# Two of the four sums of weight blocks of a seven-product group, by accumulating DMA transfers in place of VectorE

## What is computed

```
def swiglu(x, g, w_gate, w_up, w_down):
    n = rms_norm(x, g)
    return (jax.nn.silu(n @ w_gate) * (n @ w_up)) @ w_down
```

## Time and profile before

| | us |
|---|---|
| median of 3 runs | 1427.65 (1426.31 to 1430.56) |
| profiled execution, its own time | 1429.83 |
| its span | 1428.5 |
| TensorE busy | 1402.7 (98%) |
| weight loads of TensorE busy | 1321.5 (93%) |
| VectorE busy | 1061.1 (74%) |
| ScalarE busy | 713.0 (50%) |
| POOL busy | 156.6 (11%) |

### The profile page before, as it was taken

The page is one execution under the profiler, slowest core; times in us unless marked ns, Lnnn a source line. Parts: engine busy times, 40 slices in busy tenths (PEclk is TensorE's granted clock), DMA queues, the critical chain, the costliest instruction groups (busy, mean ns, idle before and its releaser), DMA issues.

```text
span 1428.5 us, 24281 instructions
## 1 busy us (share of the span) xinstructions
PE 1402.7 (98%) x9340; PEld 1321.5 (93%) x9340; DVE 1061.1 (74%) x1875; ACT 713.0 (50%) x1414; POOL 156.6 (11%) x110
## 2 busy tenths in 40 slices
PE   7999999999999999999999999999999999999998
PEld 6897878999999999999988978699999999999998
DVE  5658667878789889877444776677797998998853
ACT  5458555334355455454444685643344544544534
POOL 2416020210000000000222341102000000000002
PEclk9999999999999999999999999999999999999999
DMA  5330221233022222322233211213221223222312
GB/s 171 109 113 14 74 70 39 81 104 104 30 89 66 89 84 74 104 89 74 74 84 107 85 56 47 77 42 102 79 74 60 82 71 114 62 88 89 111 45 96
DMA packets 148642, 115.25 MB, mean 81 GB/s; under 512 B 17936, under 2 KB 143248, under 8 KB 148496
## 3 DMA queue, kind: packets, MB, share of 16 engines
q1 hardware_dynamic: 148528, 113.71, 26.4%
HBM read 108.90 MB, written 6.62 MB: 81 GB/s over the span
## 4 chain that ended last, share of the span: by engine, by line
PE 86%; DVE 7%; ACT 3%; DMA 1%; issue 1%; SPq 1%; DVEq 0%; ACTq 0%
PE ps L675 23%; PE ps L1359 13%; PE ps L1360 13%; PE ps L1361 13%; PE ps L802 3%; PE ps L804 3%; PE ps L803 3%; PE ps L1236 1%; PE ps L1127 1%; ACT pw L1521 1%; PE ps L728 1%; DMA wraw<-w_uq 1%; DVE ringl L2507 1%; PE ps L917 1%; PE ps L1153 1%
## 5 line engine op out<-in xcount | busy, mean ns | idle before, releaser
L2037 DVE TENSOR_TENSOR wlo<-wraw,whi 128x1024 fp32r<-128x1024 f32 (+2 forms) x87 | 97.6, 1122 | 122.9 <-ACT whi L1475 122.8
L1360 PE MATMUL ps<-tl,ringh 128*128 128x320 f32 x576 | 177.8, 309 | 0.0
L1361 PE MATMUL ps<-tth,ringl 128*128 128x320 f32 x576 | 177.5, 308 | 0.0
L1359 PE MATMUL ps<-tth,ringh 128*128 128x320 f32 x576 | 177.0, 307 | 0.0
L1891 ACT ACTIVATE ringh<-sums 128x512 fp32r<-128x512 f32 (+1 forms) x208 | 123.7, 595 | 106.3 <-DVE sums L2499 35.9
L2507 DVE TENSOR_TENSOR ringl<-sums,ringh 128x512 fp32r<-128x512 f32 (+1 forms) x208 | 134.2, 645 | 9.6 <-ACT ringh L1891 8.2
L1475 ACT ACTIVATE whi<-wraw 128x1024 fp32r<-128x1024 f32 (+2 forms) x87 | 81.0, 936 | 112.5 <-PE ps L675 52.0
L1360 PE MATMUL ps<-tbl,ringh 128*128 128x320 f32 x432 | 133.5, 309 | 0.0
L1361 PE MATMUL ps<-tbh,ringl 128*128 128x320 f32 x432 | 133.4, 309 | 0.0
L1359 PE MATMUL ps<-tbh,ringh 128*128 128x320 f32 x432 | 133.4, 309 | 0.0
L1359 PE MATMUL ps<-dhi,ringh 128*128 128x320 f32 x336 | 105.6, 314 | 5.2 <-DVE dlo_rest L2512 2.8
(11 more groups left out here) (431 smaller groups left out, 3786.4 us busy)
## 6 DMA issues: line engine op xcount, KB each, us to landing
raw_gate<-w_gate SPq DMA_DIRECT2D x18, 1024.0 KB, 5.4
raw_up<-w_up SPq DMA_DIRECT2D x18, 1024.0 KB, 5.3
raw_gate<-w_down SPq DMA_DIRECT2D x8, 768.0 KB, 4.2
raw_up<-w_down SPq DMA_DIRECT2D x8, 768.0 KB, 4.2
wraw<-w_down SPq DMA_DIRECT2D x16, 384.0 KB, 3.3
wraw<-w_out SPq DMA_DIRECT2D x32, 128.0 KB, 2.9
wraw<-w_out SPq DMA_DIRECT2D x16, 256.0 KB, 3.1
wraw<-w_gate SPq DMA_DIRECT2D x8, 512.0 KB, 3.9
```

Of the source, the lines that this page charges most:

```text
L1359: mm(o, wh[:, c, :], xh[:, c, :], start=fresh and c == 0, stop=False, skip_group_check=True)
L1360: mm(o, wh[:, c, :], xl[:, c, :], start=False, stop=False, skip_group_check=True)
L1361: ins = mm(o, wl[:, c, :], xh[:, c, :], start=False, stop=c == (DP if down else KH) - 1, skip_group_check=True)
L2037: vec.tensor_tensor(wlo[:, w], wraw[:, w], whi[:, w], ALU.subtract).then_inc(unit_lo.sem, 1)
```

## The change

- S1 and S3 become transfers that add to their destination, issued by POOL. For S1, a22 is added onto a21 in the raw buffer, SBUF to SBUF. For S3, SP first loads a11 a second time into a buffer (extra, load_extra), and POOL then adds a21 onto it straight from HBM.
- S2 and S4 stay with VectorE (left_sum), five products ahead in place of four. S2 is written over a11, in the raw buffer; S4 to extra.
- The signs are turned so that no weight sum has a minus: two of the results and some sums on the token side change sign, which scale = -1, subtract in place of add, or a scalar_tensor_tensor with -1 takes up again.
- In down groups other than the first of a block, products 3 and 2 change places.
- The first high part of the run waits for the last unit before it as a whole (before, for half of it, n_freed). Some semaphores are merged (tables_in into consts_in, out_copy and out_y into one).

```diff
-        yield n, 3
-        yield n, 2
+        for x in (3, 2) if n == first else (2, 3):
+            yield n, x
         yield n, 7
...
-        return {1: block_of(n, 0, 0), 2: block_of(n, 1, 0), 4: block_of(n, 1, 1), 5: sum_of(n, 0), 6: sum_of(n, 1),
-                3: sum_of(n, 0), 7: sum_of(n, 1)}[x]
+        return {1: block_of(n, 0, 0), 2: block_of(n, 1, 0), 4: block_of(n, 1, 1), 5: block_of(n, 0, 1), 6: block_of(n, 0, 0),
+                3: extra_of(n, 0), 7: extra_of(n, 1)}[x]
...
+            def load_extra(q):
+
+                n = LEFTS[q]
+                landed, value = left_landed(n)
+                sp.wait_ge(landed, value(l))
+                if q == 0:
+                    sp.wait_ge(unit_used.sem, unit_used.at(l, U_DOWN))
+                else:
+                    sp.wait_ge(a_lo.sem, a_lo.at(l, STEP[LEFTS[q - 1], 7] + 1))
+                sp.dma_start(extra_of(n, 1), left_source(l, n, 0, 0)).then_inc(pair_in[q % 2].sem, 16)
...
             for q in range(2, len(LEFTS)):
+                load_extra(q - 1)
                 load_left(q)
+            load_extra(len(LEFTS) - 1)
...
-                else:
-                    act.wait_ge(a_sum.sem, a_sum.at(l, 4 * PLACE[n] + {5: 1, 6: 2, 3: 3, 7: 4}[x]))
+                elif x in (5, 7):
+                    act.wait_ge(sum_in[x].sem, sum_in[x].at(l, 16 * (PLACE[n] + 1)))
+                else:
+                    act.wait_ge(a_sum.sem, a_sum.at(l, 2 * PLACE[n] + {6: 1, 3: 2}[x]))
...
-                    act.wait_ge(n_freed.sem, n_freed.at(l, 1))
+                    act.wait_ge(unit_used.sem, unit_used.at(l, U_DOWN))
...
-                    run(tg[:, 1, half(0)], ps[:, bx, 0:HALF], ACT.Silu).then_inc(silu_new.sem, 1)
+                    run(tg[:, 1, half(0)], ps[:, bx, 0:HALF], ACT.Silu, scale=-1.0).then_inc(silu_new.sem, 1)
...
+            def minus_sum(out, x, y):
+
+                return vec.scalar_tensor_tensor(out=out, in0=x, scalar=-1.0, in1=y, op0=ALU.mult, op1=ALU.subtract)
...
+            def left_sum(n, x):
+
+                if x == 6:
+                    dve.wait_ge(sum_in[5].sem, sum_in[5].at(l, 16 * (PLACE[n] + 1)))
+                    dve.wait_ge(a_lo.sem, a_lo.at(l, STEP[n, 1] + 1))
+                    vec.tensor_tensor(left_of(n, 6), left_of(n, 1), left_of(n, 5), ALU.add).then_inc(a_sum.sem, 1)
                 elif x == 3:
-                    vec.tensor_tensor(sum_of(n, 1), a11, a21, ALU.subtract).then_inc(a_sum.sem, 1)
+                    dve.wait_ge(a_sum.sem, a_sum.at(l, 2 * PLACE[n] + 1))
+                    if PLACE[n]:
+                        dve.wait_ge(a_lo.sem, a_lo.at(l, STEP[LEFTS[PLACE[n] - 1], 3] + 1))
+                    vec.tensor_tensor(left_of(n, 3), left_of(n, 2), left_of(n, 6), ALU.add).then_inc(a_sum.sem, 1)
...
                 for i, key in enumerate(RUN if blk else []):
+                    if i + HIGH_AHEAD < len(RUN):
+                        left_sum(*RUN[i + HIGH_AHEAD])
                     if i + AHEAD < len(RUN):
-                        left_sums(*RUN[i + AHEAD])
                         left_low(*RUN[i + AHEAD])
...
+            def add_block(x, to, block):
+
+                pool.dma_start(to, block, accum_op=ALU.add).then_inc(sum_in[x].sem, 16)
+
+            for q, n in enumerate(LEFTS):
+                landed, value = left_landed(n)
+                pool.wait_ge(landed, value(l))
+                add_block(5, left_of(n, 5), block_of(n, 1, 1))
+                pool.wait_ge(landed, value(l) + 16)
+                add_block(7, left_of(n, 7), left_source(l, n, 0, 1))
+
             sum_squares(l, ssq, 18, 14, NC_ - 1)
```

More of the change, by code:

```diff
@@ L188, in hybrid_encoder_step @@
     _, nn, _, ts = place(H0, [("skip_nn", [P, 4 * T], F32), ("nn", [P, 4, HALF], F32), ("skip_ts", [P, 4 * T], F32), ("ts", [P, 4, HALF], F32)])
-    ringh, sums2, ringl, raw_up = place(20480, [("ringh", [P, RING, KH * P], F32R), ("sums2", [P, 2, KH, P], F32),
+    ringh, extra, ringl, raw_up = place(20480, [("ringh", [P, RING, KH * P], F32R), ("extra", [P, 2, KH, P], F32),
                                                 ("ringl", [P, RING, KH * P], F32R), ("raw_up", [P, NC_, 2 * P], F32)])
@@ L421, in block_of, with extra_of, left_source @@
         return raw_of(n)[:, rows:2 * DP:2, tile * P:(tile + 1) * P]
-    def sum_of(n, i):
-        return sums2[:, i, 0:KH if n < NG else DP, :]
+    def extra_of(n, i):
+        return extra[:, i, 0:KH if n < NG else DP, :]
     def left_of(n, x):
-        return {1: block_of(n, 0, 0), 2: block_of(n, 1, 0), 4: block_of(n, 1, 1), 5: sum_of(n, 0), 6: sum_of(n, 1),
-                3: sum_of(n, 0), 7: sum_of(n, 1)}[x]
+        return {1: block_of(n, 0, 0), 2: block_of(n, 1, 0), 4: block_of(n, 1, 1), 5: block_of(n, 0, 1), 6: block_of(n, 0, 0),
+                3: extra_of(n, 0), 7: extra_of(n, 1)}[x]
+    w_gate, w_up, w_down = (a[name].rearrange("l (k p) n -> l p k n", p=P) for name in ("w_gate", "w_up", "w_down"))
+    def left_source(l, n, rows, tile):
+        if n < NG:
+            w, f = w_up if n % 2 else w_gate, PLAIN + n // 2 * 2 + tile
+            return w[l][:, KH * rows:KH * rows + KH, f * P:(f + 1) * P]
+        b, g = divmod(n - NG, KH)
+        f, d = TILE0[b + 1], 2 * g + tile
+        return w_down[l][:, f + rows:f + 2 * DP:2, d * P:(d + 1) * P]
     def down_low(first, end):
@@ L1914, in emptied @@
                         act.wait_ge(c_new.sem, c_new.at(l, C_NEW[n - 1, 7]))
-                    run(k5[:, :], ps[:, by, 0:HALF], ACT.Copy).then_inc(kept.sem, 1)
+                    run(k5[:, :], ps[:, by, 0:HALF], ACT.Copy, scale=-1.0).then_inc(kept.sem, 1)
                 elif x == 6:
@@ L2542, in down_emptied @@
                 bank = bz if x == 2 else by if x in (5, 3) else bx
-                vec.tensor_tensor(target, ps[:, bank, 0:HALF], target, ALU.add).then_inc(d_new.sem, 1)
+                vec.tensor_tensor(target, target, ps[:, bank, 0:HALF], ALU.subtract if x in (5, 7, 4) else ALU.add).then_inc(d_new.sem, 1)
                 if g == 0 and x == 1:
@@ L2591, in emptied @@
                             dve.wait_ge(d_lo.sem, d_lo.at(l, pieces_before(pair)))
-                        t1 = vec.tensor_tensor(t12[:, 0, :], tu[:, 0, half(1)], tu[:, 0, half(0)], ALU.subtract)
+                        t1 = vec.tensor_tensor(t12[:, 0, :], tu[:, 0, half(0)], tu[:, 0, half(1)], ALU.subtract)
                         if final:
@@ L2603, in emptied @@
                     dve.wait_ge(kept.sem, kept.at(l, KEPT[n, 5]))
-                    vec.tensor_tensor(dst[:, 1, half(1)], ps[:, bx, 0:HALF], k5[:, :], ALU.add).then_inc(c_new.sem, 1)
+                    vec.tensor_tensor(dst[:, 1, half(1)], k5[:, :], ps[:, bx, 0:HALF], ALU.subtract).then_inc(c_new.sem, 1)
                     if up:
@@ L2627, in emptied @@
                     dve.wait_ge(silu_new.sem, silu_new.at(l, PLAIN + SILU[2 * pair, 4]))
-                    vec.tensor_tensor(tu[:, 1, half(0)], ps[:, bx, 0:HALF], tg[:, 1, half(0)], ALU.mult).then_inc(up_c21.sem, 1)
+                    vec.scalar_tensor_tensor(out=tu[:, 1, half(0)], in0=ps[:, bx, 0:HALF], scalar=-1.0, in1=tg[:, 1, half(0)],
+                                             op0=ALU.mult, op1=ALU.mult).then_inc(up_c21.sem, 1)
                     if not in_rows:
```

72 lines of the change are left out of this document (25 added, 47 removed).

## The result

The changed kernel takes 1532.14 us (median of four runs, 1529.08 to 1534.44), against 1426.98 for the kernel before, measured beside it: ratio 1.073, 95% interval 1.070 to 1.076. It is slower by 105 us where 30 were forecast, and lies above the range. The profiled execution took 1529.08 us, span 1527.8.

What follows compares the result with a forecast made beforehand. TensorE bounds the kernel, VectorE second; after the change the weight-buffer round binds. Rounds of 318.5 us per layer minus 5 of lead, against 298.5, give +15, two layers +30: 1457 us, range 1422 to 1512.

Steps and rivals of the forecast that it cites:

- The mechanism: Weight-buffer round: next load waits behind POOL's S1 transfer and the parts; hidden below T = 3.6 us gate/up, 2.4 down.
- Relief: VectorE makes two weight sums per group instead of four; shorter TensorE waits at block starts, about -3 us.
- T: Time of POOL's transfer adding a22 onto a21, step (b) of the round: 4.35 us gate/up, 3.65 us down.
- Rival 1: POOL's transfer is hidden and only VectorE's relief counts: 1425 us; chance of hidden 0.37.
- rival 2: POOL's transfers are far slower, T = 6.1 us gate/up and 4.9 down: about 1540 us; chance 0.13.
- (c) to (g): Round after the transfer: product 5's high and low parts, bank emptying, product 6's sum, product 4's low part; 0.47 to 0.98 us each.
- the lead of 5: VectorE prepares parts four products ahead, 7 us; 5 us per layer credited, between 3 and 7, before TensorE stalls.
- DMA engines are at 0.2 to 0.3, so bandwidth is there: Added transfers and extra loads find free DMA engines; loads kept at 5.35 us gate/up and 4.2 us down.
- The transfer for product 7 is early enough: S3's block is loaded 11 products ahead, 14 us in a down group, against 10.4 us for load, addition and parts.
- dlo_first: TensorE's wait for a low part at a block's start: grows by 0.3 us, 4 x 0.3 = +1.2.
- dlo_rest: TensorE's wait for product 2's low part at block starts: vanishes with xT, -3.5 us by the waits view, -4.7 scaled.
- The likeliest case: The buffer round binds, with T from 3.9/3.3 to 5.2/4.3: 1436 to 1499 us; chance 0.50.

Runs made afterwards that it cites:

- E5: Changed kernel with both transfers kept, but product 4 of the group before placed ahead of product 5 in the order inside a group: 1449.91 us, ratio 1.015.
- E12: Changed kernel with TensorE's order and both transfers kept; only ScalarE and VectorE make product 4's parts ahead of product 5's: 1431.57 us, ratio 1.002.
- E3: Changed kernel without both adding transfers and the extra load; product 5 takes a21, product 7 takes a22: 1424.01 us, ratio 0.997.
- E4: Changed kernel with both of POOL's transfers copying instead of adding, which changes the computation: 1466.80 us, ratio 1.027.
- E2: Changed kernel without the addition for S3; the extra block is still loaded and S1's transfer stays: 1501.83 us, ratio 1.052.
- E1: Changed kernel without the addition for S1, product 5 taking a21 itself; S3's transfer stays: 1455.73 us, ratio 1.019.
- E11: Changed kernel without S3's addition, and with S1's transfer adding only two of the row blocks: 1466.54 us, ratio 1.026.

## Why the prediction was wrong, point by point

- **The mechanism was right.** "ScalarE waits before its high parts for POOL's transfer": it does in 40 of 52 groups. "Loads over 24.6 us per two groups apart": 29.4 where the earlier trace rows has 24.6. "TensorE's waits name ringl or k2s": k2s leads, though 17 times and not in every group. "POOL's issue to landing is 4 us or more": it is for gate/up. E5 and E12 show that opening this round gives 82 and 100 of 105 us back. Relief, signs, forms, semaphores and order were put at -3 us together; E3 measured a ratio of 0.997, some 4 us.
- **T was sized right**: 4.35 and 3.65 forecast; medians of 4.3 to 4.4 and 3.7 measured. The Trainium skill, DMA: Bandwidth & Descriptors (Anatomy of one DMA), would have made it 2.6 us (estimate) by its fixed time plus bytes; no transfer of 256 KB issued by POOL here is that fast, neither adding (4.3) nor copying (3.3 to 3.6 in E4). Rival 1, to which that led, is out. So is rival 2: its T of 6.1 did not come for S1, though its time (1540) is near the measured one, and POOL's issues took 1.26 to 1.44 us each beside a VectorE busy two thirds of the time. Its 6.1 was not the slowest load of that size either: the load of cache_win_v, of the same size and form, took 7.5 us.
- **What was mis-sized is the round around T.** The forecast's run of 313.5 us per layer was measured at 350.3 and 350.0 from its first matmul to its last; 36.8 + 36.5 = 73 are nearly the whole of the missing 75. Each of the 23 rounds of the table can be split in the trace: load (issue to landing), landing to POOL's start, T, and from T's landing to the next load. Sums in us per layer; the forecast's are 15 and 8 times its own terms:

| term | forecast | after, layer 0 | after, layer 1 | E2, layer 0 |
|---|---|---|---|---|
| loads | 113.9 | 130.6 | 128.0 | 119.6 |
| landing to POOL's start | 0 | 8.4 | 8.3 | 8.4 |
| T | 94.5 | 95.4 | 97.0 | 96.7 |
| the rest, (c) to (g) | 71.0 | 74.3 | 73.9 | 73.0 |
| 23 rounds | 279.4 | 308.7 | 307.3 | 297.8 |
| other three rounds and ends, less the lead of 5 | 34.1 | 41.6 | 42.7 | 38.4 |

- **The step that failed: "DMA engines are at 0.2 to 0.3, so bandwidth is there"**, by which the load stayed at 5.35 and 4.2 us in the sum. It took 5.98 and 5.12 on average in layer 0: +16.8 us per layer, the largest part of the 36.8. A mean share of the engines does not say what a load meets. E2, without S3's addition, gets 11.0 of it back and is 30 us faster; 3.4 more are that the loads of the kernel before already sum to 117.2 in layer 0, since the forecast used medians.
- **A term put at nothing**: from a load's landing to POOL's start 0.30 to 0.45 us pass, +8.4 per layer.
- **The rest** is +3.3. In 6 of the 23 rounds, at places where the loads before were 14 us apart, ScalarE was not waiting for the addition when it landed, but it or VectorE was behind with other work: +4.4. The other 17 are 1.2 below the forecast. T is +1.
- **"That lead is used up before TensorE stalls, once per layer"**: no such credit is seen. The other three rounds and the ends took 36.9 us before (300.2 - 263.3) and should have taken 34.1; they took 41.6, +7.5. A reason may be that ScalarE's bank copies and VectorE's emptyings stand in order behind the late parts; no run shows it apart.
- **"The transfer for product 7 is early enough ... 10.4 us"** of 14: the 14 are the wrong thing to set beside it. The extra buffer is single, so the chain from low part to low part must fit in one group, 9.2 us for down and 12.3 for gate/up. By the forecast's own 10.4 it does not fit for down. In E1 it was 11.55 us in the down group shown and up to 14.6 for gate/up, since the addition took up to 9.6 us beside a load and not at most 6.1, and it costs 32 us alone. In the changed kernel the S1 round hides that wait (1.0 us in all), and S3 costs through the loads instead.
- **dlo_first** grew by 0.3 us a time in E3 (0.87 from matmul starts, 0.57 before by the earlier trace rows), as forecast, and dlo_rest is gone there. In the changed kernel it is one of the names under which the late round comes out, 8.8 us in total.
- The likeliest case's own range ended at 1499, by a T of 5.2. All of the uncertainty had been put on the one unknown duration; none on the round's other terms, nor on the lead, which carried the error.

## What to carry to other kernels

When an operation goes from an engine's own queue to another place, write down the whole ring that gives a buffer back (load, landing, addition, parts, release, next load), for every buffer that the change touches. Give each step a range of its own, the steps that were there before too, for what the change sets beside them: here the load, unchanged in the program, carried more of the error than the new transfer. Compare the ring with the shortest distance between two such loads in the trace (E11), not only with the mean, nor with the time from load to use. If the ring is too long, look for what stands in it only by the order of a list: here two neighbours swapped in the order of preparation took the transfer out of the ring, and 100 of 105 us came back without touching the transfer. And be careful with credit for lead time: here 5 us per layer were taken off, and none came.

## What the runs showed of the hardware

- A DMA transfer that adds to its destination, issued by POOL: SBUF to SBUF 4.3 to 4.4 us for 256 KB, 3.7 for 192 KB (changed kernel), 3.2 to 3.3 for 128 KB (E11); from HBM 4.6 and 3.8. A plain copy by POOL takes 3.3 to 3.6 for 256 KB (E4). The adding ones took 2.6 times the copies' share of the DMA engines, in packets of 495 bytes against 3.2 KB.
- POOL is busy 1.26 to 1.44 us with an issue that adds (changed kernel) and 0.74 to 0.93 with a plain one (E4), and starts an addition onto the raw buffer 0.30 to 0.45 us after the landing that it waits for, where nothing else holds it.
- In the changed kernel a load of 1024 KB goes from 5.4 to 6.5 us into raw_gate and from 5.3 to 5.6 into raw_up, one of 768 KB from 4.2 to 5.8 into raw_gate and not at all into raw_up; the addition itself goes from 4.6 to 6.6 for gate blocks in E1. Why some loads are hit and others not is open.
- The granted clock of TensorE fell to between 0.91 and 0.99 in many 40 us stretches of the changed kernel's runs (a mixture of its two levels, 1.2 and 2.4 GHz), behind waits of up to 4.3 us on TensorE; mean 0.983. In E2, with waits as long, it was 1.00 in all stretches of the run in layer 0 and 0.96 in one of layer 1; mean 0.998. TensorE's busy time rose by 31 us for the same matmuls, and by 14 in E2, so the lower clock is behind the 31 at most in part. How much of the 105 us it makes was not tried. It did not space the loads in the 17 of 23 rounds in which ScalarE stood idle for the addition, since no step of those is TensorE's, and E2, with 0.992 to 0.998 in its runs, is still 75 us slower than before.
